# Dots' activations from a back-transposed hT, first row sums between tile one's steps, a nineteenth place, last rows in halves

## The reference, cut to what matters

```python
h2 = rmsnorm(x, norm2_g) * (1.0 + sc2) + sh2
# peer_ffn, for each of 2 tiles of 128 tokens:
q = einsum('cd,de->ce', xc, w_q)                 # 8 heads x 2 halves x 128
s = einsum('chpk,pnk->chpn', q, sub_keys)        # 128 keys per half
sv, si = top_k(s, 16)                            # per half
top_v, top_pos = top_k(sv[0][:, None] + sv[1][None, :], 16)
eid = si[0] * 128 + si[1] at top_pos             # one of 16384 experts
gate = softmax(top_v)
act = gelu(einsum('cd,chkd->chk', xc, expert_u[eid]))
y = einsum('chk,chkd->cd', gate * act, expert_v[eid])
x = x + g2 * y
return rmsnorm(x, final_g)
```

## Time and profile before

| | |
|---|---|
| median of the runs | 1248.82 us |
| profiled execution, its own time | 1249.29 us |
| its span, first to last instruction | 1247.6 us |
| TensorE / VectorE / ScalarE / GpSimd busy | 1114.3 / 862.5 / 481.3 / 471.1 us |
| gathers' queue: packets, MB | 40752, 296.24 (with the modulation weights) |
| first gather issued / last dot product starts | 580.75 / 1235.89 us |

### The profile page before, as it was taken

One profiled execution on the slowest core, in us unless ns is written; L12 is line 12 of the kernel. 1 busy time (PEld: TensorE's weight loads), 2 busy tenths in 40 slices (PEclk: granted clock), 3 DMA queues, 4 the chain that ended last, 5 costly groups with the idle time before them and its releaser, 6 DMA issues.

```text
span 1247.6 us, 14387 instructions
## 1 busy us (share of the span) xinstructions
PE 1114.3 (89%) x4792; PEld 734.1 (59%) x4792; DVE 862.5 (69%) x1929; ACT 481.3 (39%) x1118; POOL 471.1 (38%) x356
## 2 busy tenths in 40 slices
PE   4999999999999999999999999887877878778876
PEld 3899899748999998875665555323322323223222
DVE  6585568446888888756996857748668486685555
ACT  2225152044333335533635353433434334324344
POOL 0134343014544552301545555543443435444410
PEclk9999999999999998999999999998899999999998
DMA  9656675564667865464999999999999999999994
GB/s 381 264 212 237 279 270 176 229 236 167 272 274 298 322 277 209 174 260 161 403 396 395 422 421 421 421 421 422 422 421 421 421 422 421 421 421 421 422 420 193
DMA packets 57227, 413.07 MB, mean 331 GB/s; under 512 B 6480, under 2 KB 6480, under 8 KB 7120
## 3 DMA queue, kind: packets, MB, share of 16 engines
q0 software_dynamic: 40752, 296.24, 57.8%
q1 hardware_dynamic: 16272, 115.83, 23.7%
q10 hardware_dynamic: 144, 0.26, 0.1%
HBM read 411.26 MB, written 1.05 MB: 330 GB/s over the span
## 4 chain that ended last, share of the span: by engine, by line
PE 54%; DMA 31%; DVE 10%; ACT 3%; issue 1%; SPq 0%; POOL 0%; ACTq 0%; POOLq 0%; DVEq 0%
PE ps L1117 12%; DMA ring<-in_experts,idx 9%; PE ps L508 6%; PE ps L510 6%; PE ps L509 6%; DMA areaB<-in_experts,idx 6%; DMA gate_area<-in_experts,idx 5%; PE ps L549 5%; PE ps L495 3%; DMA spare<-in_experts,idx 3%; DMA mod_ring<-in_experts,idx 3%; DMA hT<-in_experts,idx 3%; PE ps L1000 2%; PE ps L769 2%; PE ps L615 2%; DMA areaB<-in_mod_w 2%
## 5 line engine op out<-in xcount | busy, mean ns | idle before, releaser
L1445 ACT ACTIVATE act<-now 128x1 f32<-128x1 f32 x256 | 50.8, 199 | 277.4 <-DVE now L2258 274.9
L1117 PE MATMUL ps<-areaB,mod_sum 128*128 128x512 f32 x248 | 124.0, 638 | 28.1 <-ACT mod_sum L1453 28.0
L1538 POOL TENSOR_TENSOR w_lo<-ring,w_hi 128x512 fp32r<-128x512 f32 x41 | 98.2, 2409 | 57.8 <-ACT w_hi L1216 57.7
L1594 POOL DMA_INDIRECT areaB<-in_experts,idx x62 | 67.4, 1087 | 132.9 <-PE ps L1117 66.9
L1703 DVE SCALAR_TENSOR_TENSOR mod_sum<-mod_ring,cols,mod_sum 128x256 f32<-128x256 f32 x280 | 116.7, 492 | 0.0
L1453 ACT ACTIVATE mod_sum<-small,act 128x128 f32<-128x128 f32 x256 | 102.8, 401 | 16.0 <-ACT act L1449 0.4
L1117 PE MATMUL ps<-ring,mod_sum 128*128 128x512 f32 x204 | 97.8, 605 | 10.4 <-ACT mod_sum L1453 10.4
L1117 PEld LDWEIGHTS ps<-areaB,mod_sum 128*128 128x128 f32 x248 | 47.2, 201 | 100.6 <-ACT mod_sum L1453 53.7
L1714 DVE TENSOR_TENSOR w_lo<-ring,w_hi 128x1536 fp32r<-128x1536 f32 x41 | 88.2, 2174 | 25.3 <-ACT w_hi L1216 25.3
L2258 DVE CUSTOM_DVE_ANT_0 areaB<-areaB,xn 128x1024 f32<-128x1024 f32 x62 | 75.2, 1223 | 42.4 <-DMA areaB<-in_experts,idx 42.2
L508 PE MATMUL ps<-hT_h,w_lo 128*128 128x256 f32 x352 | 99.4, 282 | 0.8 <-DVE hid_l L1944 0.8
(11 more groups left out here) (414 smaller groups left out, 2497.9 us busy)
## 6 DMA issues: line engine op xcount, KB each, us to landing
ring<-in_stream SPq DMA_DIRECT2D x75, 1024.0 KB, 5.9
mod_ring<-in_mod_w POOLq DMA_DIRECT2D x24, 1024.0 KB, 6.2
mod_ring<-in_mod_w SPq DMA_DIRECT2D x18, 1024.0 KB, 6.0
gate_area<-in_mod_w SPq DMA_DIRECT2D x3, 1024.0 KB, 13.5
areaB<-in_mod_w SPq DMA_DIRECT2D x3, 1024.0 KB, 23.3
gate_area<-in_stream SPq DMA_DIRECT2D x3, 1024.0 KB, 13.0
small<-in_small SPq DMA_DIRECT2D x1, 1352.0 KB, 28.3
x_sb<-in_x SPq DMA_DIRECT2D x1, 1024.0 KB, 9.3
```

Of the source, the lines that this page charges most:

```text
L1117: last = mm(ps[:, B3 + 2 * t + b, :], spread_w[n // FEW % 2][:, n % FEW, :], row[ROW_OF[n]][:, D + 512 * b:D + 512 * b + 512], start=first ...
L1538: nc.gpsimd.tensor_tensor(w_lo[s][:, HALF:], slot[s][:, HALF:], w_hi[s][:, HALF:].bitcast(F32), ALU.subtract).then_inc(lo_pool, 1)
L1594: pool.indirect_dma_start(row[ROW_OF[n]], None, experts, bass.IndirectOffsetOnAxis(ap=idx[:, n:n + 1], axis=0))\
```

## The change

- The constants: nineteen places, eleven at the start; the new one, `areas_seam`, lies over the seam of areaB and areaA (now neighbours), where the scale and shift rows were kept. Joins and queries come later in the order of rows.
- Scale and shift rows go: their spreads, broadcasts, copies, and `scale(t)`, `shift(t)`. Instead TensorE transposes hT back (`back_transposes`) into banks 7 and 1 and ScalarE copies that over xn (`h_copy`).
- `query_tile` goes; head 1's query is full width like the others and waits for `h_copy(1)`.
- The sums of rows 0 and 1 stand ahead of tile one's transposes, that of row 2 behind them; dot products 0 to 2 and `weigh` 0 to 2 are moved likewise. Two more ScalarE function switches (Exp, Gelu) are asked for early.
- Row 10 is now the one that waits for the first query of tile one (place 8); before it was row 9.
- `final_g` is loaded in front of row 64, behind `row_mm` 8.
- The last four rows are gathered as halves, u and v apart; v waits for the sum of the row twelve before and counts on that row's semaphore. VectorE makes the half indices in the last routing.
- The sums' PSUM banks are numbered `B3 + 2 * b + t` instead of `B3 + 2 * t + b`.

```diff
-EARLY = [0, 1, 2, 3, 4, 5, 6, 7, 17, 8]
-EARLY_ROWS, ROWS, ONCE = len(EARLY), 18, 17
-ROWS_BEFORE_QUERY = {1: 4, 2: 10, 3: 18, 4: 29, 5: 40, 6: 52, 7: 64}
-ROW_JOINS = {14: (9, 1), 20: (10, 2), 30: (11, 3), 42: (12, 4), 54: (13, 5), 66: (14, 6), 79: (15, 7), 80: (16, 7)}
+EARLY = [0, 1, 2, 18, 3, 4, 5, 6, 7, 17, 8]
+EARLY_ROWS, ROWS, ONCE = len(EARLY), 19, 17
+ROWS_BEFORE_QUERY = {1: 6, 2: 14, 3: 23, 4: 33, 5: 43, 6: 54, 7: 65}
+ROW_JOINS = {17: (9, 1), 28: (10, 2), 36: (11, 3), 47: (12, 4), 58: (13, 5), 70: (14, 6), 82: (15, 7), 83: (16, 7)}
+PARTED, V_LANDS_AS = EXPERTS_EACH - 4, 12
...
+            def back_transposes(t):
+                for k in range(KC):
+                    pe.wait_ge(hT_act, HT_LAST + KC * t + k + 1 if k % 4 else HT_LAST + KC * t + k + 4)
+                    last = nc.tensor.transpose(ps[:, last_bank(t, k), (k % 4) * P:(k % 4 + 1) * P],
+                                               hT[:, k, t * P:(t + 1) * P], c_("ident"))
+                    if k % 4 == 3:
+                        last.then_inc(h_T, 1)
...
             wo2_part(1, 1).then_inc(unit_done, 1)
-            broadcast_half(3, 0)
+            transposes_of(0)
             wo2_part(3, 1).then_inc(unit_done, 1)
-            broadcast_half(3, 1)
-            transposes_of(0)
+            back_transposes(0)
             wo2_part(0, 1).then_inc(unit_done, 1)
-            broadcast_half(4, 0)
             wo2_part(2, 1).then_inc(unit_done, 1)
-            broadcast_half(4, 1)
-            pe.wait_ge(hT_act, HT_LAST + KC)
-            query_tile(1, 0)
+            expert_sums(0, 2)
+            pe.wait_ge(h_ready, 2)
             transposes_of(1)
+            expert_sums(2, 3)
             first_query(1).then_inc(unit_done, 1)
...
             first_scores(1).then_inc(s_mm, 1)
+            back_transposes(1)
...
+            def h_copy(t):
+                for b in range(2):
+                    act.wait_ge(h_T, 2 * t + b + 1)
+                    A(xn[:, t, 512 * b:512 * b + 512], ps[:, last_bank(t, 4 * b), :], ACT.Identity).then_inc(h_ready, 1)
+            h_copy(0)
+            A(stat[:, 46:47], c_("ones", 0, 1), ACT.Exp)
...
             gate_exp(0)
+            A(stat[:, 62:63], c_("ones", 0, 1), ACT.Gelu)
+            weigh(0)
+            weigh(1)
             A(stat[:, 46:47], c_("ones", 0, 1), ACT.Sqrt)
-            row_copy(4, shift_row)
...
             A(stat[:, 46:47], c_("ones", 0, 1), ACT.Gelu)
+            weigh(2)
             hT_tile(1)
...
             A(score[0][:, T:2 * T], ps[:, BM, T:2 * T], ACT.Identity).then_inc(s_ready, 1)
-            for n in range(EXPERTS_EACH):
+            h_copy(1)
+            for n in range(3, EXPERTS_EACH):
...
+            def gather_v(n):
+                pool.wait_ge(row_used, n - V_LANDS_AS + 1)
+                pool.indirect_dma_start(row[ROW_OF[n]][:, D:2 * D], None, halves,
+                                        bass.IndirectOffsetOnAxis(ap=part_idx[1][:, n - PARTED:n - PARTED + 1], axis=0))\
+                    .then_inc(v_arrived(n)[0], 16)
+            gather_u(PARTED)
+            gather_u(PARTED + 1)
+            gather_u(PARTED + 2)
+            gather_v(PARTED)
+            gather_u(PARTED + 3)
+            gather_v(PARTED + 1)
+            gather_v(PARTED + 2)
+            gather_v(PARTED + 3)
...
             less_maximum(0)
-            scale(0)
+            dve.wait_ge(h_ready, 2)
+            dot_product(0)
+            normalise_gates(0)
             last_attention_residual(1, 0)
+            dot_product(1)
             last_attention_residual(1, 1)
-            shift(0)
+            dot_product(2)
             dve.wait_ge(sq_sum, 3)
             last_mean(1)
             last_norm(1)
-            dot_product(0)
-            normalise_gates(0)
-            for n in range(1, 8):
+            for n in range(3, 9):
                 dot_product(n)
-                if n == 4:
+                if n == 6:
                     route_keys(0, 1)
-                if n == 6:
-                    route_pairs(0, 1)
-                    less_maximum(1)
+            route_pairs(0, 1)
+            less_maximum(1)
...
                 if n == TOPK - 1:
-                    scale(1)
-                    shift(1)
+                    dve.wait_ge(h_ready, 4)
```

More of the change, by code:

```diff
@@ L93 @@
     USE_OF.append(ROW_OF.count(ROW_OF[_n]))
+PARTED, V_LANDS_AS = EXPERTS_EACH - 4, 12
+assert all(ROW_OF.index(ROW_OF[_n], _n) == _n and ROW_OF[_n] not in ROW_OF[_n + 1:]
+           for _n in range(PARTED - V_LANDS_AS, EXPERTS_EACH - V_LANDS_AS))
 HT_LAST = 16
@@ L1033, in raw_transposes @@
                 last.then_inc(raw_T, 1)
[L1035 to L1042, removed]
             def first_query(t, ks=range(KC)):
@@ L1063, in first_scores, with expert_sums @@
                 return last
+            def expert_sums(n0, n1):
+                for n in range(n0, n1):
+                    t = n // TOPK % NT
+                    pe.wait_ge(spread_ready, n + 1)
+                    if n >= PARTED:
+                        pe.wait_ge(*v_arrived(n))
+                    first, final = n in (0, TOPK), n >= EXPERTS_EACH - 2 * TOPK and n % TOPK == TOPK - 1
+                    for b in range(2):
+                        last = mm(ps[:, B3 + 2 * b + t, :], spread_w[n // FEW % 2][:, n % FEW, :],
+                                  row[ROW_OF[n]][:, D + 512 * b:D + 512 * b + 512], start=first, stop=final)
+                        if n == EXPERTS_EACH - 1:
+                            last.then_inc(y_done, 1)
+                    if n < EXPERTS_EACH - 1:
+                        last.then_inc(row_used, 1)
             raw_transposes(0)
@@ L1101, in head_query @@
             def head_query(h):
+                w = arrived("wq", h)
                 if h == 1:
[L1103 to L1106, removed]
+                    pe.wait_ge(h_ready, 4)
+                else:
                     pe.wait_ge(evac, 31 + h - 1)
                 gemm_T(w, h % 2, hT).then_inc(unit_done, 1)
-            def expert_sums(n0, n1):
-                for n in range(n0, n1):
-                    t = n // TOPK % NT
-                    pe.wait_ge(spread_ready, n + 1)
-                    first, final = n in (0, TOPK), n >= EXPERTS_EACH - 2 * TOPK and n % TOPK == TOPK - 1
-                    for b in range(2):
-                        last = mm(ps[:, B3 + 2 * t + b, :], spread_w[n // FEW % 2][:, n % FEW, :],
-                                  row[ROW_OF[n]][:, D + 512 * b:D + 512 * b + 512], start=first, stop=final)
-                        if n == EXPERTS_EACH - 1:
-                            last.then_inc(y_done, 1)
-                    if n < EXPERTS_EACH - 1:
-                        last.then_inc(row_used, 1)
-            done = 0
+            done = 3
             for h in range(1, HEADS):
@@ L1569, in _ @@
                 split_lo(u)
+            halves = experts.rearrange("e (h d) -> (e h) d", h=2)
             pool.wait_ge(rows_open, 1)
-            for n in range(EXPERTS_EACH):
+            for n in range(PARTED):
                 if n % TOPK == 0:
@@ L2221, in route_pairs @@
                 settled()
+                if (h, t) == (HEADS - 1, 1):
+                    final = slice(NT * TOPK - 4, NT * TOPK)
+                    for n in range(2):
+                        own(V.tensor_scalar(part_f[n], pick[1][:, final], 2.0, float(n), ALU.mult, ALU.add))
+                    settled()
+                    for n in range(2):
+                        own(V.scalar_tensor_tensor(out=part_idx[n], in0=pick[0][:, final], scalar=2.0 * P, in1=part_f[n],
+                                                   op0=ALU.mult, op1=ALU.add))
+                    settled()
                 at = NT * TOPK * h + TOPK * t
```

102 lines of the change are left out of this document (47 added, 55 removed).

## The result

The changed kernel takes 1240.68 us (median of 6 runs, 1236.98 to 1242.44) against 1248.9 for the kernel before in the same comparison (6 runs, 1248.45 to 1249.09): ratio 0.9932, 95% interval 0.9918 to 0.9946. That is 8.2 us, and outside the forecast range on the fast side.

What follows compares the result with a forecast made beforehand. Row transfers bound the kernel behind 670 us, with PE starving their queue earlier. Stalls -1.8 and last rows -1.3 sum to -3.1 us: 1246.2 from the profiled 1249.29, 1245.7 on the median's scale, range 1243.3 to 1248.0.

Steps and rivals of the forecast that it cites:

- Start of the gathers: 0: Front, up to first_scores(0): nothing PE or ScalarE works on is dropped, so the first gather's start changes by 0.
- Row 0 stays at 580.75: First gather on GpSimd: still issued at 580.75 us, as in the kernel before.
- Stalls: Early gathers, before 670 us: idle time of the slowest transfer engine goes, -1.8 us, bounds 0 to -3.6.
- one jump of the slowest engine: Between dots 14 and 31: one 0.9 us falling-behind of the trailing engine, taken out of 2.7 to leave 1.8.
- only the tail gains: Second rival, early gathers: the starved stretch just moves to rows 25 to 28, so 1247.5 us; chance 0.20.
- PE's walk: PE's early order, step by step: row 10 out near 605.4, sum 3 near 609.5, row 25 near 645.3.
- each us that sum 3 starts late: PE's bulk sums: behind 0.6 us of slack, each us of delay makes row 25 a us late on the slowest engine.
- Last rows in halves: Tail, last four rows: PE's sums limit it, residual 2.2 us after landing instead of 3.5; gain 1.3, bounds 0.3 to 2.3.
- DVE 0: DVE, early rows: 7.3 us of scale, shift and spreads go, waits replace them; worth 0 as PE is behind DVE.
- final scale 0: Final scale's load, moved to row 64: costs the same 1.24 us later in the queue, so 0.
- The slower rival: ScalarE's queue, weigh 3 behind first_query's copies and h_copy(1): PE's bulk sums start late, 1251.1 us at 6 us later; chance 0.07.
- the mean of the engines decides: Early transfer dips: the mean engine's 5.3 us counts, not the slowest's idling, giving a 5.2 gain, 1243.6 us; chance 0.15.

Runs made afterwards that it cites:

- e1: Kernel before with only the allocations of areaA and areaB exchanged, no instruction changed: 1245.18 us, ratio 0.9972.
- e9: Kernel before, areaA still first, small buffers and padding moved so areaB starts at a multiple of 1024 bytes: 1246.11 us, ratio 0.9974.
- e10: Kernel before with areaB ahead of areaA, but small buffers and padding keep areaB 96 bytes past a multiple of 1024: 1248.84 us, ratio 0.9999.
- e12: Kernel after with the last four rows gathered whole instead of as eight halves: 1240.86 us, ratio 0.9932.
- e2: Kernel after run once more, unchanged, to see how its front varies: 1241.18 us, ratio 0.9944.
- e4: Kernel after without the nineteenth place (ten at the start), areaB still ahead of areaA: 1242.57 us, ratio 0.9956.
- e11: Kernel after with PE's sums of rows 0 to 2 moved behind back_transposes(1), directly ahead of sum 3: 1244.27 us, ratio 0.9961.
- e8: Kernel after with 8 unused columns behind areaA, one scratch buffer moved into an old one; all large buffers at multiples of 64 bytes: 1242.96 us, ratio 0.9948.

## Why the prediction was wrong, step by step

**The step that failed is "Start of the gathers: 0", with its "Row 0 stays at 580.75".** It looked only at the instructions that the change takes from PE, ScalarE and DVE. The same change exchanges areaA and areaB, and with them the place of w_lo (they were neighbours before, too; their order is what is new). What stands in its place: 3.5 us from the matmuls' pace (e1, e9 and e10; e12 has the clock sum of before and its first gather 3.52 us earlier), plus a clock share that goes with the single execution (3.4 us in the profiled one, 1.7 in e1, e2 and e4, 0 in e12), and 0.8 that stay open. Nothing shows the clock share to be the change's: the same front had 8.5, 10.2 and 12.0 us in the kernel after, e2 and e12.

**Stalls: right mechanism, mis-sized, 1.8 for 3.5 to 3.9.** From the first gather to dot 32 it was 92.66 us, now 87.53; less the final scale's 1.24, that is 3.9, a little beyond the upper bound of 3.6. At the last landing 3.5 of it are left. The term was too small in two places. I took one jump of the slowest engine, 0.9, out of the 45.0 us between rows 14 and 31; by the semaphore records of the landings the changed kernel takes 42.3 there, the 17 x 2.486 of a queue that never runs dry, so all 2.7 came back. (Its dots are only 41.5 apart, because dot 14 waited for DVE and not for its row.) And row 14 itself lands 42.7 us behind the first gather instead of 43.9: the 1.2 ahead of it were in the bound and not in the term. The jump was a guess, and the upper end of the bound was the better value.

**What the stall term consists of.** At dot 31 the order alone gives 0 (e4 against e1), the place with late sums 0.4 (e11 against e1; an estimate of 2.3 had its clock not dipped), and both together 4.2 (after against e1 and e4; 2.6 in e2, whose clock dipped). Each of these is from one profile and scatters by 0.8. The place on the kernel before, with nothing else changed, was not run. The second rival, "only the tail gains", is what happens without the place: in e4 the row that waits is row 24, issued 62.7 us behind the first gather like row 25 of the kernel after.

**PE's walk** came out 1 to 2 us pessimistic. Counted from the first gather: the norm ended at 16.2 (forecast 17.15), first_query(1) at 23.2 (24.25), sum 3 started at 26.9 (28.75), row 10 went out at 23.5 (24.65), row 25 at 62.7 (64.55). Row 29 went out at 68.6 (forecast under 70.25). The residual deficit of 1.0 us was forecast as under 2. My "each us that sum 3 starts late" is confirmed at one for one by e11 (3.95 late, 3.9 longer) and by e2 (1.7 and 1.6), but the 0.6 us of slack in front of it isn't there.

**Last rows in halves: 1.3, right**, by the reason given: halves 1.25 us apart, sums 254 and 255 without a wait, no added transfer time. **DVE 0 and final scale 0** hold: the final scale's 1.24 now stands between dots 63 and 64.

**The slower rival's place was well chosen.** A clock dip at just that spot (0.75 over 4 us in e2) delayed sum 3 by 1.7 us there, and the gathers took 663.64 instead of 662.09. On the scale of the medians 3.5 + 3.5 + 1.3 is 8.3 us, and 8.2 were measured; how often such a dip comes the medians don't tell, so that the two agree this well is partly luck.

**Rival "the mean of the engines decides"** gave nearly the right stall (5.3 - 1.4 = 3.9) by a reason that the landings speak against. The slowest engine idled that long, too, and where the two come apart, in e4 against e1, the mean engine gained 1.5 us and dot 31 nothing.

## What to carry to other kernels

A line that only moves a buffer is a part of the change and needs a term: where the operands of a dense block of matmuls lie against each other in the low address bits can be worth 2% of its pace, so try a few paddings before reordering anything. An earlier order was worth nothing here until there was a further place for a row, and the two together 4 us, so price them as a pair. Work moved into an engine's wait may pay twice, if the longer wait without it drops the clock for what follows; one execution here suggests that and doesn't prove it.

## What the runs showed of the hardware

- The distance between two 128x256 matmuls with split operands depends on the buffers' positions: 116.7, 117.8, 118.8, 119.1 and 119.3 ns in otherwise equal code. One layout keeps its value, 116.7 in seven profiles, and 32 bytes change it (after and e8).
- The granted clock after 6.17 us of an idle PE was 0.50 (e11). After 2.07 us in the same place it was 1.00 in the kernel after and 0.75 in e2, so the wait alone doesn't decide.
- One program shows different clock patterns in the front from one execution to the next, 8.5 or 10.2 us in sum. A profile's front can be compared only beside its clock rows.
- Gathers of 512 KB that stood in a queue landed 1.25 us apart (1220.84, 1222.09, 1223.34 and 1224.59 in the kernel after), those of 1 MiB 2.49: cutting the last rows in two cost the transfers nothing that shows.
